# A two-layer hybrid decoder step: norm sums in column strips, short reciprocals, head sums together, decay exponentials one step earlier

## The reference, cut to what matters

```python
def _rms(x, g):
    y = x * lax.rsqrt(jnp.mean(x * x, axis=-1, keepdims=True) + EPS)
    return y * g

def _layer(x, c, ...):
    sh1, sc1, g1, sh2, sc2, g2 = split(silu(c) @ ada_w + ada_b)
    h = _rms(x, n1) * (1 + sc1) + sh1
    x = x + g1 * _mixer(h)
    h = _rms(x, n2) * (1 + sc2) + sh2
    x = x + g2 * (moe(h) if is_moe else swiglu(h))

def _mixer(h, ...):
    # windowed attention (8 heads) beside gated linear attention (4 heads)
    log_a = log_sigmoid(ga @ wa2 + ba) / 16
    g_out = _rms(gla(gq, gk, gv, log_a), gn_g) * silu(rb)     # per head of 128
    merged = sigmoid(gate_a) * (a_out @ wpa) + sigmoid(gate_b) * (g_out @ wpb)
    return merged @ w_out
```

## Time and profile before

| | us |
|---|---|
| median of 3 runs | 1976.36 (1974.95 to 1978.6) |
| the profiled execution, its own time | 1976.56 |
| its span, first to last instruction | 1975.0 |
| TensorE busy | 1837.9 (93%) |
| VectorE busy | 1021.1 (52%) |
| ScalarE busy | 830.2 (42%) |
| GpSimd busy | 112.8 (6%) |
| mean granted TensorE clock | 0.963 of 2.4 GHz |

### The profile page before, as it was taken

How to read it: one execution, slowest core, us unless ns; L and a number is a source line. 1 busy time by engine, 2 the same in 40 slices (tenths; PEclk the granted TensorE clock), 3 DMA queues, 4 the chain that set the end, 5 groups by cost and what they waited for, 6 DMA issues and landing times.

```text
span 1975.0 us, 32960 instructions
## 1 busy us (share of the span) xinstructions
PE 1837.9 (93%) x13225; PEld 1649.7 (84%) x13225; DVE 1021.1 (52%) x1376; ACT 830.2 (42%) x1211; POOL 112.8 (6%) x165
## 2 busy tenths in 40 slices
PE   6999999898999999998999998958999999999993
PEld 4888999897998999997889998947878878878872
DVE  4366554735322322335665537445576576586584
ACT  3336525323221122224365353235466465475472
POOL 1000010000101010000000100010000000000002
PEclk8999999999999999998999999988999999999995
DMA  9822234225766663224222342129577587587574
GB/s 378 337 101 86 98 137 189 86 86 190 236 231 221 237 232 122 76 85 150 68 86 87 132 183 88 53 88 364 188 296 281 184 319 272 181 326 266 184 287 140
DMA packets 96887, 362.91 MB, mean 184 GB/s; under 512 B 12196, under 2 KB 12228, under 8 KB 94976
## 3 DMA queue, kind: packets, MB, share of 16 engines
q1 hardware_dynamic: 65968, 241.07, 34.1%
q0 software_dynamic: 30800, 120.14, 17.0%
HBM read 310.80 MB, written 50.36 MB: 183 GB/s over the span
## 4 chain that ended last, share of the span: by engine, by line
PE 82%; DVE 5%; DMA 5%; ACT 4%; issue 1%; SPq 1%; POOL 0%; POOLq 0%; DVEq 0%; ACTq 0%
PE ps L626 47%; PE ps L740 16%; PE ps L758 9%; PE ps L780 2%; DMA xs<-slots 2%; PE ps L662 1%; DMA slots<-Yo_large 1%; DMA first_ada<-weights 1%; DVE mf L1882 1%; SPq L446 1%; PE ps L720 1%; PE ps L893 1%; PE ps L905 1%; PE ps L1015 1%; PE ps L700 1%
## 5 line engine op out<-in xcount | busy, mean ns | idle before, releaser
L626 PE MATMUL ps<-Hh,wh 128*128 128x260 f32 x2080 | 607.3, 292 | 22.7 <-DVE Hl L1806 17.2
L626 PE MATMUL ps<-Hl,wh 128*128 128x260 f32 x2080 | 593.7, 285 | 0.0
L626 PE MATMUL ps<-Hh,wl 128*128 128x260 f32 x2080 | 592.9, 285 | 0.0
L626 PEld LDWEIGHTS ps<-Hh,wh 128*128 128x128 f32 x2080 | 398.1, 191 | 42.6 <-issue 41.4
L626 PEld LDWEIGHTS ps<-Hl,wh 128*128 128x128 f32 x2080 | 397.9, 191 | 0.6
L626 PEld LDWEIGHTS ps<-Hh,wl 128*128 128x128 f32 x2080 | 398.0, 191 | 0.0
L1566 DVE TENSOR_TENSOR wl<-raw,wh 128x1024 fp32r<-128x1024 f32 x168 | 205.5, 1223 | 335.1 <-ACT wh L1200 334.6
L1200 ACT ACTIVATE wh<-raw 128x1024 fp32r<-128x1024 f32 x168 | 177.0, 1054 | 231.4 <-PE ps L626 228.7
L740 PE MATMUL ps<-further,XE 128*128 128x512 f32 (+1 forms) x840 | 189.8, 379 | 0.0
L740 PE MATMUL ps<-wh,XE 128*128 128x512 f32 (+1 forms) x592 | 182.7, 381 | 6.2 <-DVE XE L1680 6.2
L740 PEld LDWEIGHTS ps<-further,XE 128*128 128x128 f32 x840 | 147.2, 189 | 29.3
(11 more groups left out here) (370 smaller groups left out, 2679.3 us busy)
## 6 DMA issues: line engine op xcount, KB each, us to landing
raw<-weights SPq DMA_DIRECT2D x243, 512.0 KB, 3.4
more<-weights SPq DMA_DIRECT2D x192, 512.0 KB, 5.4
ada<-weights POOLq DMA_DIRECT2D x16, 1536.0 KB, 7.6
slots<-nothing POOLq DMA_DIRECT2D x28, 704.0 KB, 11.8
first_ada<-weights POOLq DMA_DIRECT2D x8, 2048.0 KB, 12.5
gates<-stage POOLq DMA_DIRECT2D x32, 260.0 KB, 2.8
first_ada<-weights SPq DMA_DIRECT2D x16, 512.0 KB, 16.1
g<-gates POOLq DMA_DIRECT2D x2, 3120.0 KB, 11.8
```

The source lines that it names most:

```text
L626: mm = pe.matmul(out, w, v[:, cols], start=first and q == 0, stop=last and q == 2)
```

## The change

It has five parts.

1. The square sums of the three norms after the first, `strip_sums`: the 520 columns are four quarters of 130 (`QN`), quarter j summed by 32 columns of ones into partitions 32j to 32j+31 of bank 7. Root and reciprocal then take 130 columns. `scales_spread` brings the quarters back to all partitions by four matmuls with one column of the identity repeated 128 times, into banks 4 and 5 (2 and 3 for the last norm), and VectorE reads the scales there. The eight sample columns are multiplied by the gain before this wait and not after it. The first norm of layer 0 stays as it was, but for the order of those two products.
2. The head sums: all four at once in step 32 (`head_sums`), head h in partitions 32h to 32h+31; one root, one reciprocal (step 33); `heads_spread` brings two heads at a time back (after step 34, and between the first and second slab of `br`) from one row by a row of ones. The heads' products on VectorE move into `br`. The first eight products of `br` go round two pairs.
3. A tiny root into `spare` in step 1 of `wo` and at the first down slab of the second half of `ff`.
4. The exponentials of the decay gates move from the end of step 12 into step 11, between the split and the taking of the result; the two logarithms stay in step 12 but go ahead of `exps`.
5. Five modulation products (`EARLY`) move into the second norm of layer 0, two before `scales_spread` and three after it; the first two groups of their weights are loaded at `M_made` and not at `B_read`.

```diff
+QN = N // STRIPS
+EARLY = 5
...
             for name in ("br", "wo", "ht", "ff"):
+                if name in ("ht", "ff"):
+                    turn[0] = PAIRS - 1
                 for k in range(njobs[name, l]):
-                    place_job(name, l, k)
+                    place_job(name, l, k, 2 if name == "br" and k < BR else PAIRS)
+            turn[0] = PAIRS - 1
...
-                    pool.wait_ge(sem("B_read"), 1)
+                    pool.wait_ge(sem("M_made"), KT)
                     for j in range(2):
                         load_ada(pool, j, j)
...
+            def strip_sums(rhs, first, last):
+                for j in range(STRIPS):
+                    mm = pe.matmul(ps[STRIP * j:STRIP * j + STRIP, 7, 0:QN], ones[:, 0:STRIP], rhs[:, j * QN:j * QN + QN],
+                                   start=first, stop=last)
+                return mm
+
+            def scales_spread(l, which, bank):
+                pe.wait_ge(sem("ri_made"), nth_norm(l, which))
+                for j in range(STRIPS):
+                    mm = pe.matmul(ps[:, bank + j // 2, j % 2 * QN:j % 2 * QN + QN],
+                                   ident[:, STRIP * j:STRIP * j + 1].broadcast_to([P, P]), ri[:, 0:QN], start=True, stop=True)
+                mm.then_inc(sem("ri_spread"), 1)
...
+                def head_sums():
+                    pe.wait_ge(sem("o_read"), upto("o_read", l, 1))
+                    pe.wait_ge(sem("osq_made"), upto("osq_made", l, GH))
+                    for half in range(2):
+                        for h in range(GH):
+                            mm = pe.matmul(ps[STRIP * h:STRIP * h + STRIP, 4 + half, 0:HN], ones[:, 0:STRIP],
+                                           mf[:, h, half * HN:half * HN + HN], start=True, stop=True)
+                    mm.then_inc(sem("gn_done"), 1)
+
+                def heads_spread(h0):
+                    if h0:
+                        pe.wait_ge(sem("og_made"), upto("og_made", l, h0))
+                    else:
+                        pe.wait_ge(sem("gn_ri"), upto("gn_ri", l, 1))
+                    for h in range(h0, h0 + 2):
+                        for half in range(2):
+                            mm = pe.matmul(ps[:, 4 + 2 * (h - h0) + half, 0:HN], ones[STRIP * h:STRIP * h + 1, :],
+                                           mf[STRIP * h:STRIP * h + 1, 4, half * HN:half * HN + HN], start=True, stop=True)
+                        mm.then_inc(sem(f"gb{h}_done"), 1)
...
-                    if 32 <= k < 34:
-                        head_sum(2 * (k - 32))
-                        head_sum(2 * (k - 32) + 1)
+                    if k == 32:
+                        head_sums()
+                    if k == 34:
+                        heads_spread(0)
...
-                pe.wait_ge(sem("gn_root"), upto("gn_root", l, GH))
...
+                        if br == 0 and mp == 0:
+                            heads_spread(2)
...
+                for k in range(2):
+                    next_modulation(k)
+                scales_spread(l, 1, scale_bank(l, 1))
+                for k in range(2, EARLY):
+                    next_modulation(k)
                 first_two(s0, j0, Hh, Hl, "H_made", upto("H_made", l, KT))
-                next_modulation(0)
-                next_modulation(1)
+                next_modulation(EARLY)
+                next_modulation(EARLY + 1)
...
# ScalarE
+                    if k == 11:
+                        decay_exps()          # in w1_tile, behind split_high
...
+                    if k == 12:
+                        act.activation(lab[:], lab[:], ACT.Ln, bias=1.0).then_inc(sem("lab_made"), 1)
+                        act.activation(lt[:], lt[:], ACT.Ln, bias=1.0).then_inc(sem("lt_made"), 1)
                     if 9 <= k < 17:
                         exps(k - 9)
-                    if k == 12:
-                        ...
...
                 for k in range(BR):
                     split_high(base["br", l], k)
                     if k < 2:
-                        group_high(k + 2)
+                        group_high(k)
+                    if k == 2:
+                        group_high(2)
+                        group_high(3)
...
+                    if k == 1:
+                        act.activation(spare[:], eps[:], ACT.Sqrt)
...
# VectorE
+                    if k == 33:
+                        dve.wait_ge(sem("gn_root"), upto("gn_root", l, 1))
+                        dve.reciprocal(mf[:, 4, :], mf[:, 4, :]).then_inc(sem("gn_ri"), 1)
...
                     split_low(s0, mp)
                     if mp == 0:
-                        group_normed(3)
-                    if mp < 2:
-                        group_low(mp + 2)
+                        group_normed(0)
+                        group_normed(1)
+                    if mp in (1, 2):
+                        group_normed(mp + 1)
+                        group_low(mp - 1)
+                    if mp == 3:
+                        group_low(2)
+                        group_low(3)
...
+                dve.reciprocal(ri[:, 0:QN], rt[:, 0:QN]).then_inc(sem("ri_made"), 1)
...
-            link(dve.tensor_tensor(h_s, x[:, :, T:N], bc(ri[:, T:N], KT, 1), ALU.mult))
-            link(dve.tensor_tensor(h_s, h_s, mod[:, l, gain:gain + KT, 1:9], ALU.mult))
+            link(dve.tensor_tensor(h_s, x[:, :, T:N], mod[:, l, gain:gain + KT, 1:9], ALU.mult))
+            if l or which:
+                dve.wait_ge(sem("ri_spread"), nth_norm(l, which))
+            link(dve.tensor_tensor(h_s, h_s, bc(ri_s, KT, 1), ALU.mult))
```

More of the change, by code:

```diff
@@ L151, in build @@
         eps = fixed("eps", [P, 1])
+        spare = fixed("spare", [P, 1])
         qg8 = fixed("qg8", [P, L])
@@ L399, in nth_norm, with scale_bank @@
             return 2 * l + which
+        def scale_bank(l, which):
+            return 2 if l == 1 and which == 1 else 4
         def upto(name, l, n):
@@ L1318, in norm @@
                         act.wait_ge(sem("norm_summed"), nth_norm(l, which))
[L1319 removed]
+                        act.activation(rt[:, 0:QN], ps[:, 7, 0:QN], ACT.Sqrt, bias=eps[:], scale=1.0 / D).then_inc(sem("rt_made"), 1)
                     if l == 1 and which == 1:
@@ L1485, in _ @@
                             act.activation(mf[:, h, :], z[:, Z_Q + h, :], ACT.Square).then_inc(sem("osq_made"), 1)
-                    if 32 <= k < 34:
-                        for h in range(2 * (k - 32), 2 * (k - 32) + 2):
-                            act.wait_ge(sem(f"gn{h}_done"), upto(f"gn{h}_done", l, 1))
-                            act.activation(two(mf[:, 4 + h, :]), pair(2 + h % 2), ACT.Sqrt, bias=eps[:], scale=1.0 / GV
-                                           ).then_inc(sem("gn_root"), 1)
+                    if k == 32:
+                        act.wait_ge(sem("gn_done"), upto("gn_done", l, 1))
+                        act.activation(two(mf[:, 4, :]), pair(2), ACT.Sqrt, bias=eps[:], scale=1.0 / GV).then_inc(sem("gn_root"), 1)
                     if k == 32:
@@ L1545, in _ @@
                         split_high(s0, 2 * FE + k, e * FE)
-                        next_modulation(e * EXP_SLABS + 2 * FE + k)
+                        if e and k == 0:
+                            act.activation(spare[:], eps[:], ACT.Sqrt)
+                        next_modulation(EARLY + e * EXP_SLABS + 2 * FE + k)
                         for m in range(KT):
@@ L1764, in norm @@
                     gain, shift = (3 * which + 1) * KT, 3 * which * KT
+                    if l or which:
+                        bank = scale_bank(l, which)
+                        ri_all, ri_s = pair(bank // 2), ps[:, bank + 1, HN - NS:HN]
+                    else:
+                        ri_all, ri_s = two(ri[:]), ri[:, T:N]
                     def scaled(k):
-                        dve.scalar_tensor_tensor(out=tn[:, k, 0:T], in0=x[:, k, 0:T], scalar=mod[:, l, gain + k, 0:1], in1=ri[:, 0:T],
+                        dve.scalar_tensor_tensor(out=two(tn[:, k, :]), in0=two(x[:, k, :]), scalar=mod[:, l, gain + k, 0:1], in1=ri_all,
                                                  op0=ALU.mult, op1=ALU.mult).then_inc(sem("tn_made"), 1)
@@ L1880, in group_normed @@
                 def group_normed(h):
-                    dve.wait_ge(sem("gn_root"), upto("gn_root", l, h + 1))
-                    link(dve.reciprocal(mf[:, 4 + h, :], mf[:, 4 + h, :]))
-                    link(dve.scalar_tensor_tensor(out=z[:, Z_Q + h, :], in0=z[:, Z_Q + h, :],
-                                                  scalar=sm[:, S_GN + l:S_GN + l + 1], in1=mf[:, 4 + h, :],
+                    dve.wait_ge(sem(f"gb{h}_done"), upto(f"gb{h}_done", l, 1))
+                    link(dve.scalar_tensor_tensor(out=two(z[:, Z_Q + h, :]), in0=two(z[:, Z_Q + h, :]),
+                                                  scalar=sm[:, S_GN + l:S_GN + l + 1], in1=pair(2 + h % 2),
                                                   op0=ALU.mult, op1=ALU.mult))
```

55 lines of the change are left out of this document (23 added, 32 removed).

## The result

The changed kernel takes 1944.99 us in the median (four runs, 1942.54 to 1951.23), the kernel before 1975.89 in the same session: ratio 0.9849, 95% interval 0.9829 to 0.9869. In a second session it took 1948.7 against 1976.21, ratio 0.9861 (0.9846 to 0.9876). The change makes the kernel faster by 27 to 31 us. The forecast was 1938 within 1926 to 1952. The time lies in the range, but 7 to 11 us above the forecast, and that is more than the measurement leaves open.

A forecast was written before the change was run, and what follows sets the result against it. It took TensorE, holding 82% of the chain of waits, as the bound. Terms -5.0, -7.8, -1.0, +1.5, -14.0 and -12.0 sum to -38.3, taking 1976.56 us to 1938.3, rounded 1938; range 1926 to 1952.

The forecast's parts named there:

- Square sums in strips: Sums in the wo stages and down projection: 0.57 us each instead of 0.88, 16 sums, -5.0 us.
- Rival C: Strips and one-row products do not overlap, a sum costs 2.2 us; slower than before, 1982 us, chance 0.03.
- Norm gaps: Three norm gaps: shorter root and reciprocal, less a new spread of 1.15 us; 2.6 each, -7.8 us.
- I take half of the second, -1.0: First products after norm gaps run slower; the shorter idle time wins back half of the second gap's loss, -1.0 us.
- EARLY, the mis-sized term: Five modulation products leave the stream (-3.9), but the third weight group comes late (+3.9) and clock falls (+1.5): +1.5 us.
- such a load lands 6.7 to 9.7 us after issue, median 7.6: Dense stage: landing time taken for the third group of modulation weights, putting it 17.4 us after TensorE's start.
- a gain I had set to zero: First products behind layer 0's second norm: nothing taken for the lower clock level, 13.12 us for 96 matmuls against 11.5.
- Head norm: Group norm before the branch products: cheaper sums and a stop of 0.6 us, not 6.3; 7.0 a layer, -14.0 us.
- the gates' load, issued at 323.3, lands 10.9 later: Branch stage: load starting the chain to heads 0 and 1, ready at 343.6, leaving a stop of 0.6 us.
- rival A: Branch stage: two pairs do not hold, TensorE stops some 1.5 us at each of four slabs; 1950 us, chance 0.15.
- Decay gates: Attention step: moved exponentials nearly end the wait for PT; 5.3 us in layer 0, 6.7 in layer 1, -12.0 us.
- the two loads that I had kept: Decay step: separate table loads for logarithm and next exponential, against the skill's shared set, worth some 1 us in two layers.

The follow-up runs named there:

- e: The kernel before with only the norm parts (strip sums, short root and reciprocal, spread, spare root): 1962.24 us, ratio 0.9936.
- i: The changed kernel, unaltered, measured and profiled once more: 1948.7 us.
- f: Kernel b, with GpSimd issuing the second load of gates right behind the first, not after it has landed: 1930.77 us, ratio 0.9776.
- g: Kernel b, with small unread filler products before (6) and after (12) the spread in layer 1's first norm: 1936.42 us.
- d: The kernel before with only the head norm part of the change: 1966.2 us, ratio 0.9944.
- b: The changed kernel, with GpSimd issuing the third group of modulation weights ahead of its wait for all of H_made and its memset: 1936.32 us, ratio 0.979.
- c: The kernel before with only the decay gates part of the change: 1965.12 us, ratio 0.9936.
- a: The changed kernel with part 5 undone (EARLY 0, first two weight groups loaded at the end of wo as before): 1941.56 us, ratio 0.9821.
- h: Kernel b with the edits of f and g together (gates' loads at once, filler products): 1929.22 us, ratio 0.9762.

## Why the prediction was right in sign and 7 to 11 us off

**Square sums in strips, right.** Starts in wo are 6.29 apart (0.55 a sum; 0.57 taken), and the wo and down columns give -1.6 and -1.7 for -1.6 and -1.9. Rival C's price of 2.2 a sum is far off.

**Norm gaps, right without a fall of the clock.** The reciprocal (0.97), the root (0.37) and the spread (1.16 for 1.15) are as forecast, and layer 0's gap is 2.5 shorter for 2.6 (TensorE's restarts moved from 454.00 to 442.46, 11.5, of which 9.0 was there before the gap). In layer 1's second norm TensorE's first product behind the gap starts 25.36 us after the start of the last weight split of `wo`, where it was 28.55: 3.2 shorter, about 0.6 of it from two sums, so about 2.5 for 2.6 again. The step that failed is "I take half of the second, -1.0": in layer 1's first norm nothing of the half clock goes, since the 192 matmuls still take 25.29 ( 25.11), and the spread lies inside it, 2.10. So this gap with its first products gave 1.4 for 3.6. I had named both prices, but took the one for 2.4 GHz while the earlier trace rows show the other level. That it came out right in layer 0 is owed to the modulation products in part only: e, without them, has 1.16 there too.

**EARLY, the mis-sized term.** Direction and mechanism were right: POOL's issue behind `H_made` and the memset, the third group late, half clock behind. The size was wrong, +1.5 taken and +6.5 found. Failed: "such a load lands 6.7 to 9.7 us after issue, median 7.6". In those rows two loads stood together without clears and three came singly, with two clears behind each; here two loads and four clears were issued in a row from 453.09 on, the slabs were restarting, the DMA share was 0.97, and the load took 11.0 (10.7 in i). Which of these made it slow is not separated. The issue came 0.8 later than I had it, and half clock in the 48 matmuls behind cost 2.2 where I had 1.5. The whole wait was 9.4 where I had 4 to 5. Against that stands a gain I had set to zero: the first 96 matmuls behind the gap ran at full clock.

**Head norm, right in layer 1 and short in layer 0.** -6.9 for -7.0; -5.1 for -7.0. The step "the gates' load, issued at 323.3, lands 10.9 later" failed in layer 0, where it took 12.6; the stop was 1.8 for 0.6. It was the right chain: f takes the load off it and gains 8.6. The agreement in layer 1 is partly luck: its load took 10.9 there, and where it took 11.9 (g) or 12.2 (d), the same part gained 4.5 and 4.0. The two pairs held, so rival A did not come: behind the second spread TensorE has no wait until the branch products end.

**Decay gates, right.** -4.8 and -6.2 for -5.3 and -6.7. Abs and Exp stand at 134.91 to 137.95 in ScalarE's idle time and `z` follows at 138.13; waits for `PT` are at most 0.5, but there are two in each layer where I had one, and that is the 0.5 by which each term is too large. ScalarE's timeline of step 12 has the two loads that I had kept:

```profile
148.33 1.28 ACT L1477 ACT_TABLE_LOAD   x1
149.62 0.42 ACT L1477 ACTIVATE lab<-lab 8x256 f32<-8x256 f32 x1
149.95 1.04 ACT L1478 ACTIVATE lt<-lt 128x1024 f32<-128x1024 f32 x1
151.01 1.28 ACT L1439 ACT_TABLE_LOAD   x1
```

So the rule of the Trainium skill (ScalarE: Activation LUTs, Table sets), by which one load could serve exponential and logarithm, does not show in this kernel's trace: 2.56 us of loads stand around 1.4 us of logarithms.

**What no term had.** +3.1 in a stretch of layer 0's attention that the change doesn't touch. A window of the kernel before:

```profile
303.00:307.00 4.00, 4.00 (x23) 4.00 (x23) 1.23 (x1) 1.25 (x2) 0.00 (x0) 0.57 0.17 67
```

Two of the changed kernel, over the same instructions (the slab that follows the products for `o`'s samples):

```profile
299.00:303.00 4.00, 4.00 (x21) 4.00 (x21) 0.93 (x1) 1.26 (x2) 0.00 (x0) 0.54 0.18 67
303.00:307.00 4.00, 4.00 (x24) 4.00 (x23) 0.30 (x1) 0.00 (x0) 0.00 (x0) 0.61 0.41 131
```

Near half clock in one window there, in two here. In this stretch both profiles of the changed kernel have +3.1. Of the kernels with the decay part, those that are 0.6 us or more ahead before it (the changed one, b, c, f) have +3.1 and the others (a, g, h) +0.5; the place of the stretch in time may decide, but no run tests it. The 2.8 in the experts between the changed kernel's two profiles are the stretch shown under e: 21.5 us at a clock of 0.92 in the first, 18.6 at 1.00 in the second. Stages that an edit does not touch move by 1 to 3 us in other profiles too (-1.4 and -1.5 in e; the down half, -1.8 in b, is -3.2 in f).

The parts alone add up: c, d and e are 11.8, 10.8 and 14.0 below before, 36.6 in all, and a, which holds all three, is 35.4 below. That they fit so well is partly luck, since e's 14.0 and d's 10.8 hold gains in stages that those edits do not touch. The largest piece of the distance between forecast (-38.3) and result is part 5, with 5.0 of the 7 to 11 us; the rest is the head norm of layer 0, the gap of layer 1 and the stretches of half clock.

## What to carry to other kernels

When work is moved ahead of the loads that feed it, follow the queue that issues the next load: its place in GpSimd's list (behind a wait and a memset that have nothing to do with it) was worth 12 us in its stage here, more than the 5.6 that the moved products could give. Take a load's landing time from a row in which the same traffic stands beside it, not from its median elsewhere, and from all layers, not one. And price every stop or rest of the matrix engine at its own length and again at the half clock behind it; a stop of 1.5 to 1.9 us cost 3.2 to 5.1 in the branch stage. Before a part's gain is read from a whole time, look whether it stands in the stages that the edit touches.

## What the runs showed of the hardware

A norm gap in which TensorE had only the sums and the spread (2.15 of 6.5 us busy) had a mean granted clock of 0.57, with half clock behind it, and 36 matmul records without a reader kept it at 1.00 (g). Small products did as well as fillers: five modulation products did the same in layer 0. A stop of 1.8 us between busy stretches was followed by a clock of 0.50 (the changed kernel, branch stage of layer 0), in g even one of 1.0; one of 0.3 in layer 1 of b was not. The clock also falls while TensorE counts as busy: in the windows above it is at 0.54 to 0.61 with 4.00 of 4.00 us busy, just behind 32 products of two columns (`ps<-cs,read`). How long such a stretch lasts differs between kernels whose instructions there are the same, and in the experts between two profiles of one kernel. That makes some 3 us that no edit explains, and a part alone (e) can seem to earn by its time what its own stages do not show.
